# The odd layer's mixer beside its own projection with the gates' columns last, and compression in four column groups of TensorE

## The reference, cut to what matters

```python
# layer 0 (even): compression of keys and values, among other things
blk = t[:, cmp_gather] + pe[:, None, :]            # 15 blocks of 32 tokens, 2 groups
hid = jax.nn.silu(einsum('bcgf,fh->bcgh', blk, w1))  # contraction over 32*128, 256 columns
k_c = rope(rms_norm(einsum('bcgh,hd->bcgd', hid, w2)))
# layer 1 (odd)
proj = einsum('bsd,dc->bsc', rms_norm(x), odd_w_in)  # 2048 -> 6224 columns
c_q, c_k, c_v, i_q, i_k, i_w, c_z, m_q, m_z = split_cols(proj, ODD_SPLITS)
rel = relu(einsum('bthd,bsd->bths', rope(i_q), rope(i_k)))   # 16 index heads of 64
score = einsum('bths,bth->bts', rel, w_idx)                  # top 64 keys of each query
y_c = attention(12 heads, 4 key groups, only the chosen keys)
y_m = attention(4 heads, 256 memory keys)
x = x + concat(y_c * silu(c_z), y_m * silu(m_z)) @ w_out[1]
```

## Time and profile before

| | |
|---|---|
| median of 3 runs | 3156.64 us (3154.23 to 3157.48) |
| the profiled execution's own time | 3158.29 us |
| its span, first to last instruction | 3156.5 us |
| mean granted TensorE clock | 0.986 |
| TensorE busy | 3077.3 us, 97% |
| VectorE, ScalarE, GpSimd busy | 1724.2, 1527.6, 287.6 us |
| DMA | 551.89 MB, mean 175 GB/s |

### The profile page before, as it was taken

How to read it: one execution, slowest core, us unless ns; L and a number is a source line. 1 busy time by engine, 2 the same in 40 slices (tenths; PEclk the granted TensorE clock), 3 DMA queues, 4 the chain that set the end, 5 groups by cost and what they waited for, 6 DMA issues and landing times.

```text
span 3156.5 us, 38268 instructions
## 1 busy us (share of the span) xinstructions
PE 3077.3 (97%) x14383; PEld 2572.8 (82%) x14383; DVE 1724.2 (55%) x2306; ACT 1527.6 (48%) x2121; POOL 287.6 (9%) x388
## 2 busy tenths in 40 slices
PE   8999988999979998999999999999999999999999
PEld 7888866888868887888888888888788888888887
DVE  5555537566467565544444455566675444444554
ACT  5544535454445545454444344457655344444443
POOL 1141300026200073000000000001100000000000
PEclk9999998999989999999999999999999999999999
DMA  8555530555623561556555655565455555555554
GB/s 292 175 187 191 195 110 28 187 183 188 192 84 108 186 195 46 200 175 198 187 189 182 199 187 198 188 200 174 147 175 185 192 191 189 179 193 188 198 188 145
DMA packets 256424, 551.89 MB, mean 175 GB/s; under 512 B 9296, under 2 KB 81232, under 8 KB 245552
## 3 DMA queue, kind: packets, MB, share of 16 engines
q1 hardware_dynamic: 255376, 548.72, 52.5%
q0 software_dynamic: 752, 1.48, 0.2%
q10 hardware_dynamic: 176, 0.07, 0.0%
HBM read 548.14 MB, written 2.10 MB: 174 GB/s over the span
## 4 chain that ended last, share of the span: by engine, by line
PE 58%; ACT 1%; DVE 1%; issue 0%; DVEq 0%
PE psum L1913 30%; PE psum L2041 15%; PE psum L648 10%; PE psum L2167 2%; PE psum L1882 1%; PE psum L864 0%; ACT weights_hi L469 0%; ACT rnn_gate L2205 0%; ACT rnn_decay L2204 0%; DVE weights_lo L477 0%; ACT L2204 0%; PE psum L2150 0%; PE psum L2330 0%; DVE rnn_gate L2257 0%; ACT L554 0%
## 5 line engine op out<-in xcount | busy, mean ns | idle before, releaser
L477 DVE TENSOR_TENSOR weights_lo<-weights,weights_hi 128x1024 fp32r<-128x1024 f32 (+3 forms) x1016 | 1236.3, 1226 | 1102.2 <-ACT weights_hi L469 1100.6
L469 ACT ACTIVATE weights_hi<-weights 128x1024 fp32r<-128x1024 f32 (+3 forms) x1016 | 1053.8, 1047 | 1247.9 <-PE psum L648 606.7
L648 PE MATMUL psum<-weights_hi,act_hi 128*128 128x512 f32 (+4 forms) x1952 | 755.6, 387 | 4.9 <-DVE weights_lo L477 4.8
L648 PE MATMUL psum<-weights_hi,act_lo 128*128 128x512 f32 (+4 forms) x1952 | 751.7, 385 | 0.0
L648 PE MATMUL psum<-weights_lo,act_hi 128*128 128x512 f32 (+4 forms) x1952 | 750.2, 384 | 0.0
L1913 PE MATMUL psum<-weights_hi,act_hi 128*128 128x512 f32 x1408 | 549.8, 390 | 0.0
L1913 PE MATMUL psum<-weights_hi,act_lo 128*128 128x512 f32 x1408 | 548.1, 389 | 0.0
L1913 PE MATMUL psum<-weights_lo,act_hi 128*128 128x512 f32 x1408 | 547.8, 389 | 0.0
L648 PEld LDWEIGHTS psum<-weights_hi,act_hi 128*128 128x128 f32 x1952 | 367.1, 188 | 72.3 <-issue 5.7
L648 PEld LDWEIGHTS psum<-weights_hi,act_lo 128*128 128x128 f32 x1952 | 366.6, 188 | 67.7
L648 PEld LDWEIGHTS psum<-weights_lo,act_hi 128*128 128x128 f32 x1952 | 367.1, 188 | 66.4
(11 more groups left out here) (239 smaller groups left out, 1989.0 us busy)
## 6 DMA issues: line engine op xcount, KB each, us to landing
weights<-in_ffn_w_gate SPq DMA_DIRECT2D x88, 1024.0 KB, 5.1
weights<-in_ffn_w_up SPq DMA_DIRECT2D x88, 1024.0 KB, 5.1
weights<-in_ffn_w_down SPq DMA_DIRECT2D x88, 1024.0 KB, 4.8
weights<-in_even_w_in SPq DMA_DIRECT2D x52, 956.0 KB, 4.9
weights<-in_odd_w_in SPq DMA_DIRECT2D x48, 960.0 KB, 4.8
weights<-in_w_out SPq DMA_DIRECT2D x32, 1024.0 KB, 5.0
weights<-in_rnn_w_in SPq DMA_DIRECT2D x32, 1024.0 KB, 5.3
weights<-in_attn_w_qkv SPq DMA_DIRECT2D x24, 1024.0 KB, 5.2
```

Of the source, the lines that this page charges most:

```text
L469: e.nc.scalar.activation(e.WH[(2 * slot + b) % HL][:, 0:n // 2], e.RAW[slot][:, b * n // 2:(b + 1) * n // 2], ACT.Copy).then_inc(self.hi.s ...
L477: e.nc.vector.tensor_tensor(e.WL[s][:, 0:n // 2], e.RAW[slot][:, b * n // 2:(b + 1) * n // 2], e.WH[s][:, 0:n // 2].bitcast(F32), ALU.subt ...
L648: last = e.nc.tensor.matmul(e.PS[:, banks.start + m, 0:w], a, x, start=(kk == 0 and n == 0), stop=(kk == KT - 1 and n == 2))
```

## The change

- **Odd projection.** The chunks come in an order of their own (`ODD_CHUNKS`): three chunks of 368 columns with the index heads and weights, then 512 each: k, three of q, v, the memory queries, three of the gate z, and the memory gate. They are 13 chunks and 52 slots as before.
- **The mixer** becomes a class `Odd(Pairs)` that is given to the projection as `beside`. Transposes of heads stand at 17 slots from 7 to 41 (`turns`), the 8 index units at slots 9 to 20 (`UNITS`), the rounds of the selection in VectorE's slots 23 to 31, and the attention in pairs of heads at slots 30 to 41 and of the memory at 43 to 46. A pair's scores are at slot s, its transposes at s + 1, its values at s + 2; on ScalarE and VectorE what belongs to slot s is written into slot s + 2. The barriers before, in and after the mixer are gone. Scores use one PSUM bank instead of three buffers, and so on for each step.
- **`LateGated`** multiplies by the gates on GpSimd, one piece of 512 columns at a time, and its transposes use the lead that norms use: three groups in the last chunk of the projection, one in the first of `w_out[1]`.
- **`Heads`**, for all three layers: the reduce and the scaling each come one slot earlier, the gain moves from VectorE to GpSimd, and the rotation takes 4 instructions for each half and axis instead of 6, two of them twice as wide. A semaphore counts rotated groups.
- **`compress`**: the 32 products of a half go to four column groups of 32 in turn (PSUM partitions 0, 32, 64, 96), the blocks are padded from 30 to 32 columns, and one more matmul with a constant of 32 columns adds the four groups, in place of the transpose.

```diff
...
+def spans(a, b):
+    width = 2 * -(-(b - a) // (2 * -(-(b - a) // CHUNK)))
+    return [(x, min(width, b - x)) for x in range(a, b, width)]
+EVEN_CHUNKS = spans(0, EVEN_IN)
+_index = spans(ODD["iq"], ODD["z"])
+ODD_CHUNKS = [_index[2], _index[0], _index[1]] + spans(ODD["k"], ODD["v"]) + spans(0, ODD["k"]) + spans(ODD["v"], ODD["iq"]) + \
+    spans(ODD["mq"], ODD["mz"]) + spans(ODD["z"], ODD["mq"]) + spans(ODD["mz"], ODD_IN)
+GQA_CHUNKS = spans(0, 3072)
...
-        flow.add(Gemm, evac="proj", prep=Norm(e, e.X[:], GC_NORM + KT, lead=CHUNK_LEAD), post=odd_heads(e))
-        flow.emit()
-        gated = odd_mixer(e)
-        flow = Flow(e)
-        flow.add(Gemm, evac="resid", prep=gated)
+        odd = Odd(e)
+        flow.add(Gemm, evac="proj", prep=Norm(e, e.X[:], GC_NORM + KT, lead=CHUNK_LEAD), post=odd.heads, beside=odd)
+        flow.add(Gemm, evac="resid", prep=LateGated(e, odd, [(ODD["q"], ODD["z"], 1536), (ODD["mq"], ODD["mz"], 512)]))
...
+                if self.beside is not None:
+                    self.beside.tensor(pe, 4 * c + q)
                 if c == self.last and self.next is not None:
                     self.next.prep.early_tensor(pe, q)
-                if self.beside is not None:
-                    self.beside.tensor(pe, 4 * c + q)
...
+class LateGated(Turn):
...
+    def ready(self, pe, k):
+        if k % 4 == 0:
+            pe.wait_ge(self.gated.sem, self.gated.at(k // 4 + 1))
+        if k == 4:
+            pe.wait_ge(*self.mixer.cleared())
+    def pool(self, pool):
+        e = self.e
+        for q, (val, gate) in enumerate(self.pieces):
+            pool.wait_ge(*self.mixer.final(q))
+            c = max(c for c, (x, w) in enumerate(self.chunks) if x < gate + CHUNK and gate < x + w)
+            pool.wait_ge(self.evac.sem, self.evac.at(c + 1))
+            y = e.PR[:, :, val:val + CHUNK]
+            e.nc.gpsimd.tensor_tensor(y, y, e.PR[:, :, gate:gate + CHUNK], ALU.mult).then_inc(self.gated.sem, 1)
...
+        if q == 2:
             for job in jobs:
...
-        if q == 0:
-            for job in self.of(c - 1):
-                h, w = job["v"].shape[2:]
-                gain = e.G[:, job["gain"]:job["gain"] + w].unsqueeze(1).unsqueeze(1).to_broadcast([P, MT, h, w])
-                e.nc.vector.tensor_tensor(job["v"], job["v"], gain, ALU.mult).then_inc(self.hnorm.sem, 1)
...
-            if q == 2:
+            if q == 1:
...
-            if q == 3:
+            if q == 2:
...
-                ch(dve, e.nc.vector.tensor_tensor(job["v"], job["v"], rs, ALU.mult))
+                e.nc.vector.tensor_tensor(job["v"], job["v"], rs, ALU.mult).then_inc(self.hnorm.sem, 1)
...
+                gain = e.G[:, job["gain"]:job["gain"] + w].unsqueeze(1).unsqueeze(1).to_broadcast([P, MT, h, w])
+                last = mult(job["v"], job["v"], gain)
...
-                        x1, x2 = (job["v"][:, m, :, o:o + half] for o in (2 * a * half, (2 * a + 1) * half))
...
-                        co, si = (tab(e, name, pairs, a, half, h)[:, m] for name in (cos, sin))
-                        mult(t1, x1, si)
-                        ch(pool, mult(t2, x2, si))
-                        mult(x1, x1, co)
-                        ch(pool, mult(x2, x2, co))
-                        e.nc.gpsimd.tensor_tensor(x1, x1, t2, ALU.subtract)
-                        ch(pool, e.nc.gpsimd.tensor_tensor(x2, x2, t1, ALU.add))
+                        x1, x2 = x[:, :, a, 0, :], x[:, :, a, 1, :]
+                        both = x[:, :, a]
+                        t = e.ROT[:].rearrange("p j n -> p (j n)")[:, 0:2 * h * half].rearrange("p (h x d) -> p h x d", h=h, x=2)
+                        co, si = (tab(e, name, pairs, a, half, h)[:, m].unsqueeze(2).to_broadcast([P, h, 2, half]) for name in (cos, sin))
+                        mult(t, both, si)
+                        ch(pool, mult(both, both, co))
+                        e.nc.gpsimd.tensor_tensor(x1, x1, t[:, :, 1], ALU.subtract)
+                        last = e.nc.gpsimd.tensor_tensor(x2, x2, t[:, :, 0], ALU.add)
+                        if a < pairs - 1 or m < MT - 1:
+                            ch(pool, last)
+            last.then_inc(self.roped.sem, 1)
...
-                        last = nc.tensor.matmul(e.PS[0:nb, j, 0:CMP_HID], blocks[:, j, l].rearrange("p g c -> p (g c)"),
-                                                e.RAW[q][:, k * CMP_HID:(k + 1) * CMP_HID], start=(l == 0), stop=(l == CMP_LEN - 1))
+                        x = l % quads
+                        last = nc.tensor.matmul(e.PS[32 * x:32 * x + 32, j, 0:CMP_HID], blocks[:, j, l, :],
+                                                e.RAW[q][:, k * CMP_HID:(k + 1) * CMP_HID], start=(l < quads), stop=(l >= CMP_LEN - quads))
...
-                    last = nc.tensor.transpose(e.PS[:, 2 + j, i * nb:(i + 1) * nb], hid[:, j, i * P:(i + 1) * P], e.CT[0:nb, 0:nb])
+                    last = nc.tensor.matmul(e.PS[:, 2 + j, i * nb:(i + 1) * nb], parts[:, j, i * P:(i + 1) * P], fold[:, 0:nb], start=True, stop=True)
...
+            ch(dve, nc.vector.memset(blocks[:, :, :, nb:32], 0.0))
+            ch(dve, nc.vector.tensor_reduce(fold, e.CT[:, 0:P].rearrange("p (x r) -> p r x", x=quads), AX, ALU.add))
...
-                nc.scalar.activation(hid[:, j, :], e.PS[0:nb, j, 0:CMP_HID], ACT.Silu).then_inc(e.s_gate.sem, 1)
+                nc.scalar.activation(parts[:, j, :], e.PS[:, j, 0:CMP_HID], ACT.Copy).then_inc(e.s_gate.sem, 1)
...
-                                     ACT.Copy).then_inc(e.s_gate.sem, 1)
+                                     ACT.Silu).then_inc(e.s_gate.sem, 1)
...
+class Pairs:
...
+    def tensor(self, pe, s):
+        e, nc = self.e, self.e.nc
+        if s in self.turns:
+            t, k = self.turns[s], self.order.index(s)
+            for ready in t["ready"]:
+                pe.wait_ge(*ready)
+            if k:
+                pe.wait_ge(self.hcopied.sem, self.hcopied.at(k))
+            for h in range(t["heads"]):
...
+        if s - self.VALUES in self.at:
+            n = self.at[s - self.VALUES]
+            p = self.pairs[n]
...
+            if n:
+                pe.wait_ge(self.stored.sem, self.stored.at(n))
+            for ready in p["values"]:
...
+            for i in range(2):
+                for kt in range(p["keys"] // P):
+                    last = nc.tensor.matmul(self.O(n)[:, i, :], self.PT[:, i, kt * P:(kt + 1) * P], p["v"][i][:, kt, :], start=(kt == 0),
+                                            stop=(kt == p["keys"] // P - 1))
+            last.then_inc(self.pv.sem, 1)
+        if s - self.TURN in self.at:
+            n = self.at[s - self.TURN]
+            pe.wait_ge(self.exp.sem, self.exp.at(2 * n + 2))
...
+                pe.wait_ge(self.pcopied.sem, self.pcopied.at(n))
+            for i in range(2):
+                for kt in range(self.pairs[n]["keys"] // P):
+                    at = slice(kt * P, (kt + 1) * P)
+                    last = nc.tensor.transpose(self.TP(n)[:, i, at], self.E[:, i, at], e.CT[:, 0:P])
+            last.then_inc(self.pturned.sem, 1)
+        if s in self.at:
+            n = self.at[s]
+            p = self.pairs[n]
+            for ready in p["scores"]:
+                pe.wait_ge(*ready)
+            if n:
+                pe.wait_ge(self.exp.sem, self.exp.at(2 * n))
...
+                last = nc.tensor.matmul(self.S(n)[:, i, :].rearrange("p (m k) -> p m k", k=P), p["q"][i], p["k"][i], start=True, stop=True)
+                if p["mask"] is not None:
...
+                    last = nc.tensor.matmul(self.S(n)[:, i, k0:k0 + bias.shape[-1]], e.IB[:], bias, start=False, stop=True, skip_group_check=True)
+            last.then_inc(self.score.sem, 1)
+    def scalar(self, act, s):
...
+        if s - 2 in self.at:
+            n = self.at[s - 2]
+            act.wait_ge(self.negmax.sem, self.negmax.at(n + 1))
...
+                act.wait_ge(self.pturned.sem, self.pturned.at(n))
+            for i in range(2):
+                nc.scalar.activation(self.E[:, i, 0:self.pairs[n]["keys"]], self.S(n)[:, i, :], ACT.Exp, bias=self.col(0, n)[:, i:i + 1],
+                                     accum_out=self.col(1, n)[:, i:i + 1]).then_inc(self.exp.sem, 1)
...
+    def vector(self, dve, s):
...
+        if s - 2 in self.at:
+            n = self.at[s - 2]
+            dve.wait_ge(self.score.sem, self.score.at(n + 1))
...
+                dve.wait_ge(self.stored.sem, self.stored.at(n - 3))
+            nc.vector.tensor_reduce(self.col(0, n), self.S(n), AX, ALU.max, negate=True).then_inc(self.negmax.sem, 1)
...
+class Odd(Pairs):
+    UNITS = {9: (0, 3), 10: (1, 3), 12: (0, 0), 13: (1, 0), 17: (0, 1), 18: (1, 1), 19: (0, 2), 20: (1, 2)}
+    TWICE, SELECT, ATTEND, MEMORY = 9, 23, 30, 43
...
+        turns = {7: turn(pr, c["iq"] + 768, [ready(c["iq"] + 768)]), 8: turn(pr, c["mz"], [(self.copied.sem, self.copied.at(1))], n=1),
+                 11: turn(pr, c["iq"], [ready(c["iq"])]),
```

(18 more changed lines are left out.)

412 lines of the change are left out of this document (268 added, 144 removed).

## The result

The changed kernel takes 3113.22 us (median of 4 runs, 3111.71 to 3114.15) where the kernel before takes 3156.55 (3154.23 to 3157.48). The ratio is 0.9863, with a 95% interval of 0.985 to 0.9877. The forecast was 3113.

What follows compares the result with a forecast made beforehand. TensorE, busy 3077.3 of 3156.5 us, was taken to bound the kernel. Odd layer -28, compression -11 and GpSimd before the GQA mixer -4 sum to -43, from 3156.64 to 3113 us (8 in 10: 3097 to 3136).

Steps and rivals of the forecast that it cites:

- Odd layer: Mixer moved into the projection's gemm: the 79.75 us gap leaves, 51.9 us come back, gain 28 us (20 to 36).
- Transposes of heads: Odd mixer's 66 head transposes, paid in full inside the gemm at 0.11 us each, 7.3 us.
- Index units: Odd layer's 8 units of index scores, four at 1.0 us and four at 0.6, 6.4 us.
- Attention: Odd mixer's heads and memory halves, TensorE's own cost that cannot hide: 12 x 1.83 + 8 x 1.09 = 30.7 us.
- Widths: Odd projection's new chunk widths, ten of 512 and three of 368, against twelve of 480 and one of 464: -2 us.
- Stalls: TensorE waiting in the odd layer's attention slots for late exponentials, 17 slots by 0.2 us: 4 us (0 to 12).
- about 1 us to spare: Margin between the selection's last step in VectorE's slot 31 and TensorE's first scores at its slot 30.
- Compression: Products on four column groups overlap until loads set the end: -11 us (-14 to -8; 0 without overlap).
- The rival with bare weight loads: In the compression, column groups don't overlap and weight loads stand bare: up to 3138; chance 0.13 for no overlap overall.
- GpSimd before the GQA mixer: Earlier scaling, gain on GpSimd and fewer rotation instructions cut TensorE's idle time before the mixer: -4 us (-1 to -5).
- The long chain: Rival: odd mixer's chain exceeds a slot, 33 slots wait 0.5 to 1 us more each, 3129 to 3146; chance 0.20.
- The slower one: Rival: exponentials, split and evacuation run in series on ScalarE in the odd attention, 3163 or more; chance 0.05.

Runs made afterwards that it cites:

- The run with GpSimd's wait: Changed kernel, but GpSimd waits for the selection's end before scaling and rotating the odd layer's last four query heads; 3109.13 us.

## Why the prediction was right, by its steps

The total was right and so was its order: a full attention stretch, one long gain in the odd layer, a compression that ends with its loads. That it was right to 0.3 us is luck. The odd layer gave 4.5 us less than forecast, and what filled the hole was shorter stages at a higher granted clock, for which the prediction had no term.

**Odd layer: forecast -28 (20 to 36), measured -23.5.** That is 350.97 - 326.58 = 24.4 (24.4 in the run with the old odd layer too), less 0.9 for the fourth group of gated transposes, which lies in the output projection now. Piece by piece, from the times between two insertions less 5.44 us for the granule:
- Transposes of heads: 702.80 - 696.86 - 5.44 = 0.50 for four, 8.3 in all, where I had 7.3.
- Index units: 0.87 for 128 keys (684.77 - 678.46 - 5.44) and 1.2 to 1.3 for 256, 8.3 in all, where I had 6.4. This term was mis-sized; I had taken a run of eight without its neighbours.
- Attention: 17 slots from 800.52 to 925.61 hold 30.6 us of it without the head transposes, with the first and the last about 32, where I had 30.7 and part of the 2 for switching. The unit prices from a stretch in which TensorE was full carried over.
- Widths: three chunks of 368 take 4.01 us a granule, 0.167 a matmul, so 265.8 us against 270.4: -4.6 where I took -2.
- Stalls: 5.8 us of idle time and 2.6 of clock, 8.4 where I had 4. This is the step that failed in its mechanism.

With 2.6 for three groups of gated transposes, as forecast, these come to 55.0 us of cost, where the traces have 79.75 - 24.4 = 55.4.

I had spread the stalls over 17 slots by 0.2 us each, for exponentials that come late. None came late: 99.71 of 100 us are busy, as were 22.00 of 22 in the old attention. (My text also had 7.4 us for ScalarE's worst slot and said that it doesn't fill 7.3; it does, and no wait came of it.) Instead there were two single waits, 1.43 and 4.11 us. For the larger my text had "about 1 us to spare"; I had priced the last step of the selection like a round (1.5 us), from VectorE alone, and it took 5.47 because GpSimd, to which the change gives the gains and which rotates at that moment, held VectorE up. The run with GpSimd's wait shows this: 1.34 us, and TensorE's wait is gone. For the smaller one, the copy of the index key stood in VectorE's slot 9 while TensorE asks for it at slot 8, and I had no term for it.

**Compression: forecast -11 (8 to 14), measured -11.3.** The two kernels that undo it, in part or whole, lost 11.5 and 12.0 us; in their profiles 2.5 us of the difference lie in the even mixer behind it. The mechanism was right: overlap of neighbours, then the loads. I expected three at a time and it was 0.223 / 0.067 = 3.3. (26.65 divided by the 2.38 that I had quoted is 11.2, not "some 10".)

From the first free buffer (405.00 - 0.18 = 404.82) to the products of the last granule (421.17) it was 16.35 us, where I had 1.6 + 14.8 = 16.4. But the two terms were wrong and cancel: the rates, 340 to 365 GB/s, were above my 257 to 325, and no row had shown the 1.6 us for issue and landing. The first of the four granules was there 5.8 us after its buffer came free where I had 5.3, though it moved faster; the median from issue to landing was 9.2 us, with four loads issued within 4 us, against 5.3 before. That the four slow each other is likely and not tested. The rival with bare weight loads is excluded.

The Trainium skill, "TensorE: Matmul & The Clock Gate", Part 3, lets a load overlap only matmuls of other row groups; here loads of all rows overlap products. In the first window above TensorE's products and loads are busy for 4.28 + 1.91 us of 4.90, more than the window holds. The loads overlap each other too: a load still takes 127 ns on the mean, and the time in which any is under way fell from 13.7 us to 4.2 for the same number of loads (the sum over the three windows). The ends of matmuls are modelled in these rows, but a pitch of 67 ns is also shorter than one load. So the trace speaks against that rule where loads and products use all rows.

**GpSimd before the GQA mixer: forecast -4, measured -5.2 of idle time.** I had left out that VectorE's gain of 1.2 to 1.4 us stood in the chain ahead of GpSimd and leaves it. Behind the shorter idle time the transposes and the barrier up to the scores take 5.60 us instead of 8.37 (1220.70 - 1212.33), another 2.8. Three kernels with the same idle time took 7.27 there, so this too is in part the clock of one execution. Of my term itself, GpSimd's end moved from 6.7 us behind TensorE's last matmul to 1.6, 5.1 us, where I had 3.7.

**The sum.** By the profiled executions: compression -11.3, even mixer and gated transposes -3.7, odd layer with its output projection -23.5, GQA idle time -5.2, the projections ahead of it -0.2, GQA transposes -2.8, start +1.4, rest -0.4: -45.7, which is 3156.5 - 3110.8. The start is no effect of the change: the compression's first transposes lie between 399.77 and 401.58 us in all profiles. Between medians it is -43.3; the profiled execution of the kernel before was 1.7 us above its median and that of the changed kernel 0.5 below.

**The rivals.** The long chain lost nothing in the attention. The slower one needed 2.5 us a slot and is far off. "Nothing else is as late" ahead of the GQA mixer was right to 0.4 us.

## What to carry to other kernels

A stretch in which an engine is full gives unit prices that survive a move into another stage; a stretch in which it is not gives prices without its neighbours. When work moves to GpSimd, price VectorE's steps beside it with GpSimd running, and put the one step that others wait for where GpSimd is idle: one wait instruction was worth 4 us here. When loads set the end, more parallelism in the engine buys nothing: two column groups did what four did. And a stage that got shorter without a reason in the edit is not yet a gain: here single profiles of kernels that are the same up to that stage differ by 2.6 us in it, with the clock they were granted.

## What the runs showed of the hardware that I had not expected

Some of VectorE's operations slow down a lot beside GpSimd: a pair of casts from 0.43 to 2.53 us, of scalings by a constant from 0.42 to 1.51, of sums from 0.49 to 1.43, two split halves from 2.36 to 4.52 and 5.48. Its maxima and replacements don't: the pair of MAX8 took 0.61 us with GpSimd running (it is busy for 6.84 of the 7 us from 763) and 0.61 or 0.62 without, and the replacement over 256 columns 0.41 either way.

```profile
763.59 0.61 DVE L2027 MAX8 stats<-proj 128x8 f32<-128x128 f32 x2
...
764.57 0.41 DVE L2028 MATCH_REPLACE8 proj<-stats,proj 128x256 f32<-128x256 f32 x1
...
768.33 0.61 DVE L2027 MAX8 stats<-proj 128x8 f32<-128x128 f32 x2
```

GpSimd is slowed as well, 14.2 us for a chain that took 12.3 with VectorE's splits gone. The Trainium skill, "SBUF — State Buffer", section "Who interferes with whom", gives this rule: the two engines share a pair of ports, which one holds for a whole instruction, and VectorE needs it for two operands in SBUF or in its two-port modes. The trace agrees: the slow ones are those, and the maximum, with one operand, is not. The replacement's row names two tensors and it isn't slowed; the list in that section has neither operation.

In the second half of the compression 16 instructions over four column groups take 1.94 us at a granted clock of 0.50 and over two groups 1.92 us at 1.00. TensorE waits more between buffers with four, and its clock fell from 1.00 to 0.50 there (to between 0.50 and 0.59 in the other seven profiles with four groups, in windows of 9 to 11 us). So at half clock four groups do per microsecond what two do at full clock.
